# Half as many slots per expert, two passes over the weights, and half of each down matrix unsplit

## The reference

```python
def grouped_moe(h, router_w, router_b, w_gate, w_up, w_down):
    scores = jax.nn.sigmoid((h @ router_w).astype(jnp.float32))
    ...
    _, idx = lax.top_k(masked, TOP_K)          # TOP_K = 2
    wts = jnp.take_along_axis(scores, idx, axis=-1)
    wts = wts / jnp.sum(wts, -1, keepdims=True)
    gate = jnp.sum(jax.nn.one_hot(idx, N_EXPERTS, dtype=jnp.float32) * wts[..., None], axis=-2)
    out = jnp.zeros_like(h)
    for e in range(N_EXPERTS):
        hid = jax.nn.silu(h @ w_gate[e]) * (h @ w_up[e])
        out = out + gate[..., e:e + 1] * (hid @ w_down[e])
    return out
```

## Time and profile before

| | |
|---|---|
| runs (us) | 2124.3, 2129.81, 2131.21; median 2129.81 |
| the profiled execution, own time | 2134.72 us |
| its span in the trace | 2133.5 us |
| mean granted TensorE clock | 0.957 of full speed |
| PE / DVE / ACT / POOL busy | 1988.0 / 1411.6 / 1146.0 / 133.1 us |
| DMA queue of the weights | 59.2% of 16 engines' span |

### The profile page before, as it was taken

How to read it: one execution, slowest core, us unless ns; L and a number is a source line. 1 busy time by engine, 2 the same in 40 slices (tenths; PEclk the granted TensorE clock), 3 DMA queues, 4 the chain that set the end, 5 groups by cost and what they waited for, 6 DMA issues and landing times.

```text
span 2133.5 us, 31616 instructions
## 1 busy us (share of the span) xinstructions
PE 1988.0 (93%) x13268; PEld 1790.3 (84%) x13268; DVE 1411.6 (66%) x1663; ACT 1146.0 (54%) x1576; POOL 133.1 (6%) x152
## 2 busy tenths in 40 slices
PE   4879899999989889999998899999999899999998
PEld 4767799999888679999997779988998877998997
DVE  5576688888756668888886546556556536566555
ACT  3465477777636547777774444434444534444443
POOL 0000111111000011111100000000000000000000
PEclk8989899999999989999999989999999989999999
DMA  7324498899943248988895425564664423654652
GB/s 223 106 85 139 158 304 276 294 306 296 298 123 114 84 158 279 308 281 291 296 304 178 139 87 170 179 197 158 198 182 156 151 87 119 199 196 159 198 179 98
DMA packets 317715, 413.40 MB, mean 194 GB/s; under 512 B 16352, under 2 KB 249568, under 8 KB 317568
## 3 DMA queue, kind: packets, MB, share of 16 engines
q1 hardware_dynamic: 316480, 409.72, 59.2%
q10 hardware_dynamic: 1088, 1.57, 0.3%
HBM read 409.43 MB, written 1.84 MB: 193 GB/s over the span
## 4 chain that ended last, share of the span: by engine, by line
PE 77%; DVE 9%; ACT 5%; DMA 3%; issue 2%; POOL 0%; ACTq 0%; DVEq 0%
PE PS L387 13%; PE PS L390 13%; PE PS L391 13%; PE PS L379 8%; PE PS L383 8%; PE PS L380 8%; DVE weights_lo L364 3%; PE PS L1342 3%; PE PS L1389 2%; ACT weights_hi L359 2%; PE PS L406 1%; DMA weights_raw<-in_w_up 1%; DMA weights_raw<-in_w_down 1%; PE PS L402 1%; PE PS L1817 1%
## 5 line engine op out<-in xcount | busy, mean ns | idle before, releaser
L364 DVE TENSOR_TENSOR weights_lo<-weights_raw,weights_hi 128x1024 fp32r<-128x1024 f32 x752 | 884.8, 1219 | 311.4 <-ACT weights_hi L359 308.6
L359 ACT ACTIVATE weights_hi<-weights_raw 128x1024 fp32r<-128x1024 f32 x752 | 750.5, 1048 | 209.1 <-PE PS L391 119.6
L379 PE MATMUL PS<-hT_hi,weights_hi 128*128 128x256 f32 (+1 forms) x1488 | 433.5, 291 | 27.5 <-ACT weights_hi L359 18.2
L383 PE MATMUL PS<-hT_hi,weights_lo 128*128 128x256 f32 (+1 forms) x1488 | 429.7, 289 | 2.6 <-DVE weights_lo L364 2.6
L380 PE MATMUL PS<-hT_lo,weights_hi 128*128 128x256 f32 (+1 forms) x1488 | 429.6, 289 | 0.0
L387 PE MATMUL PS<-weights_hi,hT_hi 128*128 128x256 f32 (+2 forms) x1312 | 394.9, 301 | 3.0 <-ACT weights_hi L359 1.9
L390 PE MATMUL PS<-weights_lo,hT_hi 128*128 128x256 f32 (+2 forms) x1312 | 390.8, 298 | 0.8 <-DVE weights_lo L364 0.8
L391 PE MATMUL PS<-weights_hi,hT_lo 128*128 128x256 f32 (+2 forms) x1312 | 390.6, 298 | 0.0
L379 PEld LDWEIGHTS PS<-hT_hi,weights_hi 128*128 128x128 f32 (+1 forms) x1488 | 291.0, 196 | 36.6 <-issue 17.2
L383 PEld LDWEIGHTS PS<-hT_hi,weights_lo 128*128 128x128 f32 (+1 forms) x1488 | 290.6, 195 | 4.3 <-DVE weights_lo L364 3.8
L380 PEld LDWEIGHTS PS<-hT_lo,weights_hi 128*128 128x128 f32 (+1 forms) x1488 | 291.3, 196 | 1.8
(11 more groups left out here) (293 smaller groups left out, 2540.2 us busy)
## 6 DMA issues: line engine op xcount, KB each, us to landing
weights_raw<-in_w_in SPq DMA_DIRECT2D x80, 1024.0 KB, 5.6
weights_raw<-in_w_gate SPq DMA_DIRECT2D x64, 1024.0 KB, 6.0
weights_raw<-in_w_up SPq DMA_DIRECT2D x64, 1024.0 KB, 5.4
weights_raw<-in_w_down SPq DMA_DIRECT2D x64, 1024.0 KB, 5.7
weights_raw<-in_w_ff SPq DMA_DIRECT2D x64, 1024.0 KB, 5.6
weights_raw<-in_w_branch SPq DMA_DIRECT2D x12, 1024.0 KB, 5.0
weights_raw<-in_w_o SPq DMA_DIRECT2D x8, 1024.0 KB, 5.0
weights_raw<-in_ple_gate SPq DMA_DIRECT2D x8, 1024.0 KB, 6.6
```

What stands on the lines that cost most here:

```text
L359: act.activation(u.flat[0][:, c:e], u.x[:, c:e], ACT.Copy).then_inc(*sig.mark("w_hi", u.u, i))
L364: dve.tensor_tensor(u.flat[1][:, c:e], u.x[:, c:e], u.flat[0][:, c:e].bitcast(F32), ALU.subtract).then_inc(*sig.mark("w_lo", u.u, i))
L379: pe.matmul(o, w[0], x[0], start=start, stop=False)
L383: return pe.matmul(o, w[1], x[0], start=False, stop=stop)
```

## The change

- `SLOTS` is 64. The high and low parts of 64 slots lie side by side as one stationary operand of 128 columns, so a product has two passes (over the high and the low part of the weights), and the two halves of its 128 output rows are the parts still to be added.
- The pick serves four experts at a time (`GROUP`), its banks are emptied by plain copies, alternately on ACT and DVE; there are 16 small gate matmuls.
- Gate units and up units are 512 columns wide and hold 4 k each, loaded in runs of 8 KB a partition instead of 1 KB, in the order gate 0, gate 1, up 0, up 1.
- ACT copies gate and up out of PSUM; eight float32 matmuls with a matrix `fold` (the identity twice) transpose them and add the two parts; silu, product and split come after it, 128x256 each. The gate factor is applied when the down result is split.
- Down half 1 is not split: four float32 matmuls read the raw buffer, 64 rows by 512 columns. Its buffer is free for the next load when PE has done this product.
- The adds of half 1 use 64 rows; `h` is split with another striding; the constants have 64 more columns.
- In the opening unit 0 is loaded before the tables, units 1 and 2 behind them. The other small parameters (`small_sync`) are issued before unit "mla 0", between unit 3 and the parameters of the first mixer. The angles and sines of the first table move into the bias steps (12 to 13), with other counts in `take_steps`.

```diff
+SLOTS = P // 2
+GROUP = 4
...
-        for i in range(2 if e < N_EXP else 0):
-            for n in ("gate", "up"):
-                w = a["w_" + n][l, e][:, 256 * i:256 * i + 256]
-                plan.append((f"{n} {e} {i} {l}", w.rearrange("(k p) n -> p k n", p=P), KD, 256))
+        for n in ("gate", "up") if e < N_EXP else ():
+            for i in range(2):
+                w = a["w_" + n][l, e].rearrange("(p k) n -> p k n", p=P)
+                plan.append((f"{n} {e} {i} {l}", w[:, 4 * i:4 * i + 4, :], 4, 512))
...
+                self.native = self.name.startswith("down") and self.name.split()[2] == "1"
...
-                sp.wait_ge(*sig.at("w_lo", u.u - NRAW, 1))
+                former = units[u.u - NRAW]
+                sp.wait_ge(*(sig.at("ps", former.name) if former.native else sig.at("w_lo", former.u, 1)))
...
         def split_scalar(act, u):
+            if u.native:
+                return
...
         def tables_sync(sp):
-            sp.dma_start(const[:, :], a["consts"]).then_inc(*sig.landing("tables_in"))
             for i, name in enumerate(("positions", "positions_2")):
                 sp.dma_start(pos_i[:, i, :], a[name].rearrange("a s -> (a s)").partition_broadcast(P)).then_inc(
-                    *sig.landing("tables_in", "all"))
-            sp.dma_start(relb[:, :, :], a["bias_rows"]).then_inc(*sig.landing("small_in"))
+                    *sig.landing("tables_in"))
+            sp.dma_start(relb[:, :, :], a["bias_rows"]).then_inc(*sig.landing("tables_in"))
+            sp.dma_start(const[:, :], a["consts"]).then_inc(*sig.landing("tables_in", "all"))
+
+        def small_sync(sp):
...
             for i in range(16):
+                if i == 13:
+                    angles(0)
...
+            def pick(group):
+
+                pe.wait_ge(*sig.at("moe_pool", n_(f"columns {group}")))
+                for k in range(KD):
+                    b = banks.take(pe, n_(f"pick {group} {k}"), "dve_took" if k % 2 else "act_took", among=4)
+                    for part in range(2):
                         for t in range(NT):
-                            for part in range(2):
-                                last = pe.matmul(PS[:, b, j * S:(j + 1) * S],
-                                                 h_split[part][:, t, (kk + j) * P:(kk + j + 1) * P], to_slot[:, t, :],
-                                                 start=t == 0 and part == 0, stop=t == 1 and part == 1)
-                    last.then_inc(*sig.mark("ps", n_(f"pick {pair} {kk}")))
-                b = banks.take(pe, n_(f"pick gate {pair}"), "dve_took", among=4)
+                            last = pe.matmul(PS[:, b, part * S:(part + 1) * S], h_split[part][:, t, k, :],
+                                             to_slot[:, t, :, :].rearrange("p e s -> p (e s)"), start=t == 0, stop=t == 1)
+                    last.then_inc(*sig.mark("ps", n_(f"pick {group} {k}")))
+                b = banks.take(pe, n_(f"pick gate {group}"), "dve_took", among=4)
+                for j in range(GROUP):
+                    for c in range(2):
+                        for t in range(NT):
+                            e_ = GROUP * group + j
+                            last = pe.matmul(PS[SLOTS * c:SLOTS * c + SLOTS, b, j:j + 1], to_slot[:, t, j, :].bitcast(F32),
+                                             gate[:, t, e_:e_ + 1], start=t == 0, stop=t == 1)
+                last.then_inc(*sig.mark("ps", n_(f"pick gate {group}")))
...
+            def two_pass(o, x, u, w, start, stop, fresh):
+
+                pe.matmul(o, x, w[0], start=start, stop=False)
+                if fresh:
+                    lo_ready(pe, u)
+                return pe.matmul(o, x, w[1], start=False, stop=stop)
+
+            def up(e_, which):
+
+                b = banks.take(pe, n_(f"{which} {e_}"), "act_took", among=4)
...
+                for i in range(2):
+                    name = n_(f"{which} {e_} {i}")
+                    u = use(pe, name)
+                    for k in range(4):
+                        last = two_pass(PS[:, b, :], x_e[i][:, k, e_ % GROUP, :, :].rearrange("p c s -> p (c s)"), u,
+                                        at_k(u.pair, k, 0, 512), i == k == 0, i == 1 and k == 3, k == 0)
+                    last.then_inc(*sig.mark("ps", name))
...
+                pe.wait_ge(*sig.at("act_took", n_(f"up {e_}")))
                 for j in range(2):
-                    for t in range(NT):
-                        last = pe.matmul(PS[:, b, j:j + 1], to_slot[:, t, j * P:(j + 1) * P].bitcast(F32),
-                                         gate[:, t, 2 * pair + j:2 * pair + j + 1], start=t == 0, stop=t == 1)
-                last.then_inc(*sig.mark("ps", n_(f"pick gate {pair}")))
-
-            def up(e_, i):
-                b = banks.take(pe, n_(f"up {e_} {i}x"), "dve_took", among=4)
-                if e_ % 2 == 0 and i == 0:
-                    pe.wait_ge(*sig.at("dve_took", n_(f"pick {e_ // 2} 6")))
-                for j, which in enumerate(("gate", "up")):
-                    name = n_(f"{which} {e_} {i}")
-                    u, s0 = use(pe, name), P * (e_ % 2)
-                    for k in range(KD):
-                        last = rows_still(pe, PS[:, b, j * 256:(j + 1) * 256], u, at_k(x_e, k, s0, s0 + P),
-                                          at_k(u.pair, k, 0, 256), k == 0, k == KD - 1, k == 0)
-                    last.then_inc(*sig.mark("ps", name))
-
-            def turn_hidden(e_):
-                b = banks.take(pe, n_(f"turn {e_}"), "dve_took", among=4)
-                pe.wait_ge(*sig.at("dve_took", n_(f"up {e_} 1x")))
-                for j in range(4):
-                    last = transpose(pe, PS[:, b, j * P:(j + 1) * P], hids[e_ % 2][:, j * P:(j + 1) * P])
+                    for c in range(4):
+                        last = pe.matmul(PS[:, b, (4 * j + c) * SLOTS:(4 * j + c + 1) * SLOTS],
+                                         gate_up[e_ % 2][:, j, c * P:(c + 1) * P], fold, start=True, stop=True)
...
+                if half == 1:
+                    u = units[place[name]]
+                    pe.wait_ge(*sig.at(f"raw{u.raw}_loaded", u.u))
+                    for k in range(4):
+                        last = pe.matmul(PS[0:SLOTS, b, :], hidT[:, SLOTS * k:SLOTS * k + SLOTS], u.x[:, 512 * k:512 * k + 512],
+                                         start=k == 0, stop=k == 3)
+                    last.then_inc(*sig.mark("ps", name))
+                    return
...
+                    last = two_pass(PS[:, b, :], hid_e[e_ % 2][:, k, :, :].rearrange("p c s -> p (c s)"), u,
+                                    at_k(u.pair, k, 0, 512), k == 0, k == 3, k == 0)
...
+            def gate_or_up(e_, j, which):
+                feed(n_(f"{which} {e_} 0"), n_(f"{which} {e_} 1"))
+                act.wait_ge(*sig.at("ps", n_(f"{which} {e_} 1")))
+                act.activation(gate_up[e_ % 2][:, j, :], PS[:, banks.of(n_(f"{which} {e_}")), :], ACT.Copy).then_inc(
+                    *sig.mark("act_took", n_(f"{which} {e_}")))
...
+                act.activation(sil, PS[:, banks.of(name), 0:256], ACT.Silu).then_inc(*sig.mark("moe_act", n_(f"silu {e_}")))
+                act.wait_ge(*sig.at("dve_took", name))
+                hi_part(act, hid_e[e_ % 2][:, :, 0, :], hidT.rearrange("p (k s) -> p k s", k=4)).then_inc(
+                    *sig.mark("moe_act", name))
...
+                dve.wait_ge(*sig.at("moe_act", n_(f"silu {e_}")))
+                dve.tensor_tensor(hidT, sil, PS[:, banks.of(name), 256:512], ALU.mult).then_inc(*sig.mark("dve_took", name))
                 dve.wait_ge(*sig.at("moe_act", name))
-                lo_part(dve, hid_e[1][:, :, :], one_bank(banks.of(name), 4), hid_e[0][:, :, :]).then_inc(
-                    *sig.mark("dve_took", name))
+                lo_part(dve, hid_e[e_ % 2][:, :, 1, :], hidT.rearrange("p (k s) -> p k s", k=4),
+                        hid_e[e_ % 2][:, :, 0, :]).then_inc(*sig.mark("moe_dve", n_(f"hidden {e_}")))
...
+                dve.scalar_tensor_tensor(y_e[1][0:n, :], PS[0:n, banks.of(name), :],
+                                         gate_of(e_ // GROUP)[0:n, e_ % GROUP:e_ % GROUP + 1], y_e[0][0:n, :].bitcast(F32),
+                                         ALU.mult, ALU.subtract).then_inc(*sig.mark("dve_took", name))
...
             if name == "mla 0":
+                if l == 0:
+                    small_sync(sp)
                 up_params(sp, l)
...
-            for u in units[0:first]:
+            load_unit(sp, units[0])
+            tables_sync(sp)
+            for u in units[1:first]:
                 load_unit(sp, u)
-            tables_sync(sp)
```

188 lines of the change are left out of this document (90 added, 98 removed).

## The result

The changed kernel takes 2167.55 us (median of 2166.32 to 2174.17) where the kernel before takes 2130.44 on the same chip: a ratio of 1.0182, 95% interval 1.0156 to 1.0208. The forecast was 2140 with a range of 2060 to 2178; the time lies inside the range and outside the likeliest case's own range (2125 to 2158), at the lower edge of rival B's (2165 to 2200). The profiled execution has a span of 2167.5 (own time 2168.7).

The account below looks back on a forecast made before the run. PE paced the expert loops at 21.5 us an expert; afterwards the load ring would. Loops −7.6, opening +3 and clock +15 make +10.4 on the median of 2129.8: 2140 us, range 2060 to 2178.

Parts of the forecast that it names:

- the likeliest case: Whole kernel: the forecast of 2140 us itself, own range 2125 to 2158, chance 0.31.
- rival B: Expert loops: the clock falls in nearly every round, +40 to +75, 2165 to 2200 us, chance 0.18.
- The ring: Expert loops: buffer free, load, split, use, starting from down half 1's buffer; 20.9 us a round, 24.2 with the pick.
- the wait of 2.6: Expert rounds: the longest of PE's three waits, near 1, 1 and 2.6 us, 4.6 idle of 20.9.
- The clock's price: Expert loops: a third of the 22 rounds without pick lose 2.0 us each to clock falls, +15, ends 0 and 75.
- below 0.95: Expert loops: a sign named for the forecast, the granted clock of the loops under 0.95.
- The ends of the loops: Each expert loop: 27.1 us to the end of the first down, 15 for the last expert.
- The opening: Before the expert loops: reordered small loads, constants and the sines' chain cost +3 us, ends −2 and +7.
- the 38: Opening: the prediction is wrong if the bias matmuls begin after 47 or before 38 us.
- C: Expert loops: the clock stays and the ring is as priced, −4.6, 2125 us (2114 to 2138), chance 0.22.
- D: Expert loops: ring shorter than PE's work, PE keeps the pace at 16.3 a round; −119, 2006 us, half 2066, chance 0.22.
- E: Expert loops: up 0 and up 1 share the DMA engines, both landing near 7.6; +2.2 a round, 2187 us, chance 0.05.

Follow-up runs that it names:

- own_raw: The changed kernel with a fourth raw buffer, kept for the unsplit down units, the other five units turning in three: 2077.01 us, ratio 0.9761 to the kernel before.
- split_both: The changed kernel with down half 1 split again and multiplied in two passes, still three raw buffers: 2122.5 us, ratio 0.996 to the kernel before.
- fill_gate: The changed kernel with three idle full-precision 128-column matmuls ahead of each expert's gate product: 2166.04 us.
- fill_down: The changed kernel with three idle full-precision 128-column matmuls ahead of each unsplit product of down half 1: 2190.86 us.
- fill_nopick: The changed kernel with three idle matmuls in each of the two waits before down half 0, except in rounds with the pick: 2154.17 us.
- early_product: The changed kernel with gate copy, silu and product put ahead of the split of up 1 on ACT and DVE: 2167.04 us.
- own_early: own_raw with gate copy, silu and product put ahead of the split of up 1 on ACT and DVE: 2114.9 us, ratio 0.993 to the kernel before.
- own_split: The changed kernel with a raw buffer of its own for down half 1, which is also split and multiplied in two passes: 2081.61 us, ratio 0.9764.

## Why the prediction came out as it did

**The ring was right.** Its length of 20.9 us, its links, the buffer that starts it, and that it eats PE's whole saving are in the trace and in own_raw, split_both, fill_gate and fill_down. The 28 rounds were put at 605.0 and +15 for the clock; they took 311.0 + 314.1 = 625.1. Of the 5.1 above the forecast, 1.6 are in the rounds without the pick (476.4 for 459.8 + 15) and 3.4 in those with it (148.6 for 145.2). What was wrong inside the round is how it divides: PE's work was put at 16.3 and is 17.4 where it runs on (own_raw's 18.1 less 0.7), in part because the unsplit product takes 3.65 for 3.5 and the turn 2.0 for 1.6; and the wait of 2.6 that was to stand in each round is nowhere. So PE's busy time fell by 50.4 and not by 128 − 15 = 113. While the ring is the pace this costs nothing.

**The clock's price came out right in the rounds, in part by luck, and was left out at their ends.** I took a third of the 22 rounds without the pick at 2.0, 7 falls and 15 us in all. It was 10 of these 22, at 1.7, so 17: more falls than I took, each smaller, and none behind a wait of 2.6. What I had not counted are the fall before the first down (1.7) and the one in a tail (5.4): 24.1 in all. That the waits bring the falls on is shown by fill_nopick; why early_product and own_early, with waits as long at other places of the round, have 2 and none stays open. The granted clock of the whole loops was 0.96 and 0.97, not below 0.95 as I had named it.

**The ends of the loops were mis-sized.** From the start of a loop to the end of the first down I had 27.1; it took 30.5 and 28.0, +4.3 together. The tail was put at 15 and took 23.8 and 17.8, +11.6, of which 5.4 are that fall of the clock; the last expert's chain of copy, product, split and add (waits of 1.60, 1.55 and 1.93 there) has no gate and up products of a next expert beside it to hide behind. This is the largest term in error. The experiments did not test it; it is read from the trace.

**The opening.** +3 was taken and +2.5 measured, and undoing it changes nothing; the bias matmuls began at 37.47, just before the 38 that I had named as a sign of error, for POOL's copies began at 32.0 instead of 33.2, although the load of w_ukv was issued at 26.9 instead of 25.6. So the first masks came 2.5 sooner and the loop still began 2.5 later. Part of it is behind the angles, which took DVE 7.3 us where I had 6.0 and leave PE waits of 1.64 and 2.48; the waits for masks ahead of them had also grown, to 2.47 (at 51.99). Before, the longest behind the first was 1.63. Only some 1.0 of the 2.5 is the opening's: with the old opening the loop began 1.5 later than before all the same.

**Between the loops** I had nothing and the trace has +5.1. PE is busy 2.9 more there than before at a granted clock of 0.90 against 0.92, and in steps of 1 us the falls of the clock there cost 14.7 against 12.3. PE also stands still longer between the last add of the loop and its first matmul behind it (the last add ends at 615.2):

```profile
620.90 3.88 PE L411 MATMUL PS<-const 128*128 128x128 f32 x16 [5.66 <-DVE h L580]
```

Before, this wait was 3.30. It is 5.4 to 5.9 in all the runs in which the unsplit product shares the three buffers, and 2.9 to 3.3 in own_raw, own_early, own_split and split_both. The wait and the falls together are 4.8 of the 5.1. From last add to first gate matmul it was 200.8 before, 204.8 after, 201.6 in own_raw's execution and 202.8 to 205.3 in those of split_both, fill_gate and fill_down. What makes the wait and the falls differ was not settled.

The sum: opening −0.5, rounds +5.1, first stretches +4.3, tails +11.6, between the loops +5.1, rest −2.0, together +23.6 above the span forecast (2143.9 against 2167.5). The other 4 of the 27.5 us are the distance from the profiled execution to the median, 4.9 taken from the kernel before and 1.2 in the changed one.

**The rivals.** B (falls in nearly every round) gives the right time for the wrong reason: 10 of 28 rounds had a fall, and heads, tails and the stretch between the loops fill the gap. C's clock did not stay. D was wrong for the changed kernel, and what it needed is what own_raw made: with a fourth buffer and none that waits for PE a round is 18.1, PE is the pace and the kernel 2.4% faster than before. It did not reach D's 16.3, as PE's own work is 17.4. E did not happen, up 0 landed 5.3 after its issue with up 1 right behind it. The rule that was weighed for the clock ("TensorE: Matmul & The Clock Gate" of the Trainium skill, section "A second HAM failure mode: psum-queue depth-cycling") held in kind: short idle times between groups of matmuls went with 11 falls of the clock, and filling two of them in a round took 8 away. The estimate from "DMA: Bandwidth & Descriptors" of the Trainium skill, 4.4 us for a unit, was too low here by 0.9: the load that mattered took 5.3, on another issue path than the section's.

## What to carry to other kernels

When work is moved off an engine that copies and onto the one that consumes, ask what the copy had freed: here the split released a load buffer 3.4 us after it began, and without it the buffer was held until a product at the end of the round was done. Follow one buffer around, from the release to the issue, the landing, the work and the next release; if that circle is longer than the work of the busiest engine, it is the pace, and a quicker engine only waits. Then one buffer can be worth more than the instructions that are saved (90 us here, where PE's saved work gave nothing), and the sum should price the head and the tail of the loop with the same care as its rounds.

## What the runs showed of the hardware

The falls of the clock came in pieces of 4 to 5 us worth 1.7 us each, mostly at the end of a round and the start of the unsplit product, behind waits of 0.83 and 0.93, and 1.3 us of idle matmuls in these waits removed 8 of 11. Waits as long elsewhere in the round were not followed by falls: own_early has 0.46, 0.96 and 0.56 in each and no fall in its rounds. Loads of 1 MB moved at 284 GB/s with a DMA share of 0.77 when the gate and up units came in runs of 8 KB a partition, and at 272 with 0.79 in runs of 2 KB, and in this ring that was 24 us of 2167. Sixteen gate matmuls of one column with 64 output rows took 1.12 (819.9 − 818.7), four with 128 rows 0.95.
